# Gathering the rows of an expert as half rows on 128 partitions, and turning them with four transposes

## The chip, the cores and the metric

The kernel runs on one core of a Trainium2 chip, in float32. The metric is the device time of one execution in microseconds. The time before is the median of three executions.

## What is computed

One transformer block over 512 tokens of width 1024: a mixer (attention and a recurrent branch), and then a mixture of 32 experts, from which each token uses two. Only the second half is touched by the change:

```python
group_sel = jnp.argmax(group_logits, axis=-1)
top_p, top_i = lax.top_k(jax.nn.softmax(in_group, axis=-1), TOP_K_IN_GROUP)   # 2 of the 8 experts of a group
...
for e in range(N_EXPERTS):                                                     # 32
    hid = jax.nn.silu(t @ w_up1[e]) * (t @ w_up3[e])                           # 1024 -> 512, twice
    y = y + combine[:, e:e + 1] * (hid @ w_down[e])                            # 512 -> 1024
return y.reshape(b, s, d)
...
x = x + gt2 * rmsnorm(y, norm_gains[l, 3])
```

The weights of one expert are 6.3 MB (two matrices of 1024x512 and one of 512x1024), 201 MB for all of them.

## The kernel before

**Blocks.** The expert part works in blocks of at most 64 tokens (CAP) of one expert; with these inputs there are 32 blocks, one for each expert, and up to 18 more would be run if an expert had more than 64 tokens. There are three sets of buffers for the weights (u = 0, 1, 2), used in turn. Three blocks are written out, a loop `Fori` runs three blocks in each pass, and the last two are written out again.

**Weights.** SP issues all weight loads on one queue. The loads of the block three further on are issued when the block that holds the buffers has passed them: first halves at `up_half`, second halves at `up_done`, and the down matrix at `down_done` (L476, L480, L484). The first sets are issued ahead of the routing, the last three pieces of set 2 (L550, L551) after `rows_moved`, which stands for the rows of block 0.

**Rows.** When a tile of 128 tokens is ready, ACT scales it (L1031) and stores it into a buffer in DRAM, `h2_dram`, 512 rows of 1024 floats. The rows of block 0 are picked by matmuls with a one-hot matrix (L2168) and copied by ACT and DVE into `hrow[0]`. For every other block POOL gathers the 64 rows with an indirect DMA (`gather_rows`, L668) into `hrow[u]`, 64 partitions of 1024 floats; the indices are in `idx_i`. An index out of bounds leaves its row as it is, so a block with 20 tokens gathers 20 rows. The gather for the block three further on is issued when PE has turned the rows that are in the buffer (`hg_done`).

**Turning.** `turned(u)` (L2189) brings the rows to 128 partitions of the model's width with eight transposes, each of 64 rows by 128 columns (every eighth column of a row), into PSUM bank 0; DVE scales and shifts the eight pieces into `hgT` (L1503). PE does this for the next block between the up matmuls (L2211) and the down matmuls (L2230) of the present one. The outputs go back to token order by matmuls (L2195), which DVE adds to `acc` (L1544).

**End.** After the last blocks but two, SP loads `h2_dram` back (L590), 128 partitions by 1024 floats for each of four tiles. ACT (L1069) and POOL (L698) multiply it by the standard deviation in place, which gives x1 again; POOL (L702) and DVE add it to the outcome, and SP stores it.

## Time and profile before

| | us |
|---|---|
| median of three executions | 1099.11 |
| lowest, highest | 1097.51, 1099.91 |
| span of the profiled execution, first to last instruction | 1095.7 |
| PE busy in it | 1028.6 |
| DVE busy | 665.0 |
| ACT busy | 326.2 |
| POOL busy | 167.4 |

The profile gives the span of the profiled execution and not its whole time; the median of the timed executions lies 3.4 us above the span. PE's busy time is that of modelled ends of pipelined matmuls, so it doesn't say that PE is at its limit. What matters beside it is the busy share of the 16 DMA engines in each stretch and the GB/s that they moved.

### The profile page before, as it was taken

To read this page: it belongs to the slowest core of one execution; us is meant where nothing else is said; L and a number is where in the kernel's file an instruction comes from. 1 tells how busy PE (TensorE), PEld (TensorE's weight loads), DVE (VectorE), ACT (ScalarE), POOL (GpSimd) and SP (SyncE) were. 2 spreads that over 40 slices of the span, in tenths; PEclk is the share of its full clock that TensorE was granted. 3 is DMA by queue.
4 is the path that set the end of the run, shared out by engine and by line. 5 is a ranking of instruction groups with operands and counts; after the bars stand their busy time and mean duration, and the time that the engine had idled before them with its cause. 6 is when DMAs were issued, how large, how long until landed. Compare 5 with 4: busy or idle time off the path is not lost.

```text
span 1095.7 us, 18202 instructions
## 1 busy us (share of the span) xinstructions
PE 1028.6 (94%) x7403; PEld 591.1 (54%) x7403; DVE 665.0 (61%) x1131; ACT 326.2 (30%) x500; POOL 167.4 (15%) x220
## 2 busy tenths in 40 slices
PE   3999999999999999999998999999999999889895
PEld 1588588755557677768884444444334333333332
DVE  2478768444457443238347777777776665666666
ACT  4342462366652223365351111111111101110114
POOL 0100000322220011264500200000000000001003
PEclk9999999999999999999999999999999999999998
DMA  9676303205320004243439999999999999999994
GB/s 342 245 242 217 136 28 127 77 13 180 115 77 2 3 4 157 72 155 123 172 122 407 376 396 401 400 402 399 407 404 408 404 404 395 405 396 402 411 423 196
DMA packets 67732, 275.22 MB, mean 251 GB/s; under 512 B 7742, under 2 KB 17256, under 8 KB 43098
## 3 DMA queue, kind: packets, MB, share of 16 engines
q1 hardware_dynamic: 62976, 263.84, 62.4%
q10 hardware_dynamic: 2218, 6.52, 1.6%
q0 software_dynamic: 2480, 4.01, 1.3%
q8 instruction: 46, 0.75, 0.3%
q14 instruction: 12, 0.10, 0.0%
HBM read 274.26 MB, written 4.21 MB: 254 GB/s over the span
## 4 chain that ended last, share of the span: by engine, by line
PE 45%; SPq 25%; DVE 13%; DMA 7%; ACT 5%; issue 3%; POOL 1%; DVEq 0%; ACTq 0%
SPq L476 17%; PE ps L2211 8%; SPq L480 5%; PE ps L2230 4%; PE ps L1878 3%; DMA ring<-in_w_in 3%; DMA arena<-in_w_up 2%; SPq L484 2%; PE ps L2195 2%; PE ps L1859 2%; DMA arena<-in_w_mod 2%; PE ps L1867 2%; PE ps L1979 2%; PE ps L1860 1%; PE ps L1861 1%
## 5 line engine op out<-in xcount | busy, mean ns | idle before, releaser
L1544 DVE TENSOR_TENSOR arena<-arena,ps 128x1024 f32<-128x1024 f32 x124 | 145.5, 1215 | 52.9 <-PE ps L2195 52.9
L2211 PE MATMUL ps<-arena 128*64 128x512 f32 x672 | 152.9, 596 | 12.0 <-DMA arena<-in_w_up 11.2
L2211 PEld LDWEIGHTS ps<-arena 128*64 128x64 f32 x672 | 47.5, 137 | 105.5 <-issue 99.8
L1054 ACT ACTIVATE results<-ps,ST 64x512 fp32r<-64x512 f32 x64 | 43.8, 685 | 182.8 <-PE ps L2230 182.4
L2211 PE MATMUL ps<-ring,arena 128*64 128x512 f32 x352 | 79.9, 597 | 6.9 <-DMA ring<-in_w_up 5.5
L1047 ACT ACTIVATE arena<-ps 128x256 f32<-128x256 f32 x32 | 12.3, 385 | 234.7 <-PE ps L2211 234.7
L1720 PE MATMUL ps<-h_upper,w_upper 128*128 128x512 f32 (+1 forms) x184 | 73.7, 401 | 4.8 <-POOL h_lower_first L604 4.6
L2230 PE MATMUL ps<-arena 128*64 128x512 f32 x336 | 76.7, 598 | 1.3 <-DMA arena<-in_w_down 1.3
L1554 DVE SCALAR_TENSOR_TENSOR results<-ps,ST,results 64x512 fp32r<-64x512 f32 x64 | 48.0, 749 | 47.4 <-ACT results L1054 46.9
L2195 PE MATMUL ps<-results,back 128*128 128x512 f32 x248 | 73.7, 419 | 0.0
L1722 PE MATMUL ps<-h_upper,w_lower 128*128 128x512 f32 (+1 forms) x184 | 72.1, 392 | 0.0
L1503 DVE TENSOR_SCALAR arena<-ps,par 128x64 f32<-128x64 f32 x256 | 67.1, 335 | 0.1
L2195 PEld LDWEIGHTS ps<-results,back 128*128 128x128 f32 x248 | 42.1, 190 | 30.6 <-issue 23.5
L1867 PE MATMUL ps<-arena,ring 128*128 128x512 f32 x128 | 56.9, 597 | 0.0
L690 POOL COPY ST<-ST 128x1 f32 x27 | 4.9, 182 | 331.6 <-DVE results L1554 331.6
L2211 PEld LDWEIGHTS ps<-ring,arena 128*64 128x64 f32 x352 | 23.8, 137 | 57.3 <-issue 43.0
L1721 PE MATMUL ps<-h_lower_first,w_upper 128*128 128x512 f32 (+1 forms) x138 | 54.3, 394 | 0.0
L2230 PEld LDWEIGHTS ps<-arena 128*64 128x64 f32 x336 | 22.9, 136 | 44.6 <-issue 37.5
L2189 PEld LDWEIGHTS ps<-cst,arena 64*128 64x128 f32 x256 | 30.6, 200 | 24.5 <-issue 24.3
L1720 PEld LDWEIGHTS ps<-h_upper,w_upper 128*128 128x128 f32 (+1 forms) x184 | 34.3, 186 | 15.5 <-issue 6.7
L613 POOL TENSOR_SCALAR_AFFINE_SELECT arena<-arena 128x128 f32<-128x128 f32 x64 | 32.3, 537 | 66.2 <-DVE arena L1249 48.4
L2230 PE MATMUL ps<-ring,arena 128*64 128x512 f32 x176 | 40.2, 598 | 1.4 <-DMA ring<-in_w_down 0.9
(424 smaller groups left out, 1866.7 us busy)
## 6 DMA issues: line engine op xcount, KB each, us to landing
arena<-in_w_up SPq DMA_DIRECT2D x84, 1024.0 KB, 28.1
ring<-in_w_up SPq DMA_DIRECT2D x44, 1024.0 KB, 27.7
ring<-in_w_down SPq DMA_DIRECT2D x11, 2048.0 KB, 32.4
arena<-in_w_down SPq DMA_DIRECT2D x11, 2048.0 KB, 31.4
arena<-in_w_down SPq DMA_DIRECT2D x20, 1024.0 KB, 27.2
ring<-in_w_mod SPq DMA_DIRECT2D x6, 2048.0 KB, 9.1
arena<-in_w_mod SPq DMA_DIRECT2D x6, 2048.0 KB, 9.5
ring<-in_w_in SPq DMA_DIRECT2D x6, 2048.0 KB, 8.4
```

The lines of the kernel that those rows point to most:

```text
L476: eng.dma_start(eset_up[u][i][:, 2048 * m:2048 * m + 2048], src).then_inc(w_in_sem[u][m], 16)
L480: eng.dma_start(dst, src).then_inc(w_in_sem[u][m], 16)
L1503: last = TS(hgT[:, k, :], ps[:, 0, CAP * k:CAP * k + CAP], V("A1", k), V("SH1", k), ALU.mult, ALU.add)
L1544: TT(two_banks(acc[:, t, :]), two_banks(acc[:, t, :]), ps[:, BACK_BANK[t]:BACK_BANK[t] + 2, :], ALU.add).then_inc(back_added, 1)
L1554: last = STT(yo[o:o + HD, h:h + 512], ps[a:a + HD, DOWN_BANK, :], weight[a:a + HD, :], yo[a:a + HD, h:h + 512].bitcast(F32), ALU.mult, ALU ...
L1720: mm(ps[0:m_, b, :], hi, h_hi[:, k, :], start=(k == 0), stop=False)
L1721: used = mm(ps[0:m_, b, :], hi, h_lo[k], start=False, stop=False)
L1722: last = mm(ps[0:m_, b, :], lo, h_hi[:, k, :], start=False, stop=(k == KD - 1))
L1867: last = mm(ps[:, bank, :], w[:, k, P * (n % 2):P * (n % 2) + P], hT[:, k, :], start=(k == 0), stop=(k == KD - 1))
L2195: ins = mm(ps[:, bank + h, :], back[:, u, P * t:P * t + P], yo[:, 512 * h:512 * h + 512], start=True, stop=True)
L2211: last = mm(ps[64 * hf:64 * hf + 64, UP_BANK, :].rearrange("p (m n) -> p m n", m=2), hgT[:, k, :], up_pair(u, k)[:, :, 256 * hf:256 * hf + ...
L2230: last = mm(ps[64 * hf:64 * hf + 64, DOWN_BANK, :], hv2[:, k % 2, k // 2, :], wd[:, k % 2, 512 * hf:512 * hf + 512], start=(k == 0), stop= ...
```

## The change

`h2_dram` is stored in half order: the model's column 8p + 4g + j stands at place 512g + 4p + j of its row, so that each row is two half rows of 512 floats, g = 0 and g = 1. A gather reads 128 half rows, those with g = 0 into partitions 0 to 63 and those with g = 1 into 64 to 127; the index of a half row is twice the token's number, plus g. A block's rows are then 128 partitions by 512 floats, and are turned by four transposes of 128x128. The copy into `h2tok`, the one-hot matmuls for block 0 and the copies behind them follow the order, and the end reads the order back. A constant of one column (`nohalf`) is added, and one clearing of 128x1024 on POOL is left out. Loads of weights, waits and semaphores stay.

```diff
-        idx_i = sb("idx_i", [CAP, MAXB], I32)
-        idx_now = sb("idx_now", [CAP, NSET], I32)
+        idx_i = sb("idx_i", [P, MAXB], I32)
+        idx_now = sb("idx_now", [P, NSET], I32)
...
-        hrow = [S(14, 1)[0:CAP, 0:D], S(14, 1)[0:CAP, D:2 * D], S(13, 1)[0:CAP, D:2 * D]]
+        hrow = [S(14, 1)[:, 512 * u:512 * u + 512] for u in range(NSET)]
+        by_halves = lambda a: a.rearrange("t (p g j) -> t g p j", g=2, j=4)
+        h2_halves = h2_dram.rearrange("t (g n) -> (t g) n", g=2)
...
-        x1_rows = [S(i)[:, 0:D] for i in (0, 1, 15, 16)]
+        h2_rows = [S(i)[:, 0:D] for i in (0, 1, 15, 16)]
+        x1_rows = [S(i)[:, D:2 * D] for i in (0, 1, 15, 16)]
+        h2_by_column = [a.rearrange("t (g p j) -> t p g j", g=2, j=4) for a in h2_rows]
+        x1_by_column = [a.rearrange("t (p g j) -> t p g j", g=2, j=4) for a in x1_rows]
...
                 nc.gpsimd.indirect_dma_start(
-                    out=hrow[u], out_offset=None, in_=h2_dram, in_offset=bass.IndirectOffsetOnAxis(ap=index, axis=0),
-                    bounds_check=T - 1, oob_is_err=False).then_inc(hrow_in[u], 16)
+                    out=hrow[u], out_offset=None, in_=h2_halves, in_offset=bass.IndirectOffsetOnAxis(ap=index, axis=0),
+                    bounds_check=2 * T - 1, oob_is_err=False).then_inc(hrow_in[u], 16)
...
-                nc.gpsimd.tensor_scalar(x1_rows[t], x1_rows[t], std2[:, t:t + 1], None, ALU.mult).then_inc(x1_back, 1)
+                nc.gpsimd.tensor_scalar(x1_by_column[t], h2_by_column[t], std2[:, t:t + 1], None, ALU.mult).then_inc(x1_back, 1)
...
-                link(A(h2tok[:, t % 2, :], x1[:, t, :], ACT.Copy, scale=V("rs", 8 + t)))
+                link(A(h2tok[:, t % 2, :].rearrange("t (g p j) -> t g p j", g=2, j=4), by_halves(x1[:, t, :]), ACT.Copy,
+                       scale=V("rs", 8 + t)))
...
-                    A(x1_rows[t], x1_rows[t], ACT.Copy, scale=std2[:, t:t + 1]).then_inc(x1_ready, 1)
+                    A(x1_by_column[t], h2_by_column[t], ACT.Copy, scale=std2[:, t:t + 1]).then_inc(x1_ready, 1)
...
-                    last = TS(hgT[:, k, :], ps[:, 0, CAP * k:CAP * k + CAP], V("A1", k), V("SH1", k), ALU.mult, ALU.add)
+                    at = P * (k % 4) + CAP * (k // 4)
+                    last = TS(hgT[:, k, :], ps[:, 0, at:at + CAP], V("A1", k), V("SH1", k), ALU.mult, ALU.add)
...
-                    last = mm(ps[CAP * h:CAP * h + CAP, 0, :], picked[:, t, :], x1[:, t, 512 * h:512 * h + 512], start=(t == 0), stop=(t == NT - 1))
+                    last = mm(ps[CAP * h:CAP * h + CAP, 0, :], picked[:, t, :], by_halves(x1[:, t, :])[:, h], start=(t == 0), stop=(t == NT - 1))
...
-                hv = hrow[u].rearrange("p (q k) -> p k q", k=KD)
-                for k in range(KD):
-                    last = tr(ps[:, 0, CAP * k:CAP * k + CAP], hv[:, k, :], ident[0:CAP, 0:CAP])
+                hv = hrow[u].rearrange("s (p j) -> s j p", j=4)
+                for j in range(4):
+                    last = tr(ps[:, 0, P * j:P * j + P], hv[:, j, :], ident)
```

On POOL's queue this is the place from the clearing ahead of the first gathers to the clearing of `acc` behind them. Line numbers of the kernel before; `arena` holds `hrow`, and `h_rows` is `h2_dram`.

```order
L662 MEMSET arena 128x2048
L663 MEMSET arena 128x1024
L668 DMA arena<-h_rows,idx_i 64x1024 x2
L675 TENSOR_LOAD nblk_i
L675 ISA x2
L678 MEMSET arena 128x2048
L679 MEMSET arena 128x2048
```

In the changed kernel the same place reads as follows, with its own line numbers (five to seven higher).

```order
L668 MEMSET arena 128x2048
L673 DMA arena<-h_rows,idx_i 128x512 x2
L680 TENSOR_LOAD nblk_i
L680 ISA x2
L683 MEMSET arena 128x2048
L684 MEMSET arena 128x2048
```

Nothing changed its place: one clearing is gone, and each gather has 128 rows of 512 floats where it had 64 rows of 1024. It is the same in the loop and for the last two blocks.

On PE's queue this is the start of block 0, with the turning for blocks 0 and 1, in the kernel before; `results` holds the outputs of an expert.

```order
L2168 MATMUL ps<-arena 64x512 x8
L2176 MATMUL ps<-arena 64x50 x16
L2189 MATMUL ps<-cst,arena 128x64 x8
L2249 MATMUL ps<-key_diagonals,cst 128x512 x2
L2211 MATMUL ps<-ring,arena 64x512 x16
L2241 MATMUL ps<-SAs,arena 64x50 x16
L2189 MATMUL ps<-cst,arena 128x64 x8
L2218 MATMUL ps<-cst,arena 128x128 x2
L2230 MATMUL ps<-ring,arena 64x512 x8
```

And in the changed kernel, with its own line numbers (seven higher):

```order
L2175 MATMUL ps<-arena 64x512 x8
L2183 MATMUL ps<-arena 64x50 x16
L2196 MATMUL ps<-cst,arena 128x128 x4
L2256 MATMUL ps<-key_diagonals,cst 128x512 x2
L2218 MATMUL ps<-ring,arena 64x512 x16
L2248 MATMUL ps<-SAs,arena 64x50 x16
L2196 MATMUL ps<-cst,arena 128x128 x4
L2225 MATMUL ps<-cst,arena 128x128 x2
L2237 MATMUL ps<-ring,arena 64x512 x8
```

Only the two turnings differ: eight transposes to 64 columns each are four to 128 columns each, at the same place.

## Rows read from the trace of the kernel before

**Rows 1.** The page, part 2: the span in 40 equal slices, 27.4 us each.

```profile
DMA  9676303205320004243439999999999999999994
GB/s 342 245 242 217 136 28 127 77 13 180 115 77 2 3 4 157 72 155 123 172 122 407 376 396 401 400 402 399 407 404 408 404 404 395 405 396 402 411 423 196
```

**Rows 2.** Busy time by stretch: length, PE, PEld, DVE, ACT, POOL, clock, DMA share, GB/s.

```profile
640.00:840.00 200.00, 200.00 (x936) 82.14 (x936) 144.43 (x265) 24.57 (x42) 18.30 (x42) 1.00 1.01 402
840.00:1010.00 170.00, 154.02 (x704) 62.31 (x700) 108.74 (x192) 18.91 (x32) 14.14 (x32) 1.00 1.02 403
1020.00:1060.00 40.00, 38.54 (x180) 16.10 (x178) 25.79 (x48) 3.90 (x7) 0.00 (x0) 1.00 1.01 422
```

**Rows 3.** Waits of PE from 600 to 1070 us: us in total, times, longest.

```profile
PE ps L2211 <- DMA arena<-in_w_up: 11.2, 11, 1.8
PE ps L2211 <- DMA ring<-in_w_up: 5.5, 10, 1.2
```

**Rows 4.** The chain that ended last, two blocks in turn: start us, us, what.

```profile
629.69 3.43 PE ps L2211 x16
...
643.82 3.43 PE ps L2211 x16
```

**Rows 5.** The DMA view of the run: gather queue (packets, MB, share of engines), gathers issued.

```profile
q0 software_dynamic: 2480, 4.01, 1.3%
...
arena<-h_rows,idx_now POOLq DMA_INDIRECT x27, 7.2
...
arena<-h_rows,idx_i POOLq DMA_INDIRECT x4, 7.6
```

**Rows 6.** The DMA view from 640 to 1010 us: the gather queue.

```profile
q0 software_dynamic: 1975, 3.07, 3.0%
```

**Rows 7.** Busy time by stretch around two gathers, and one stretch of small packets.

```profile
881.00:884.00 3.00, 3.00 (x19) 1.97 (x16) 1.28 (x4) 0.39 (x1) 0.00 (x0) 1.00 1.02 350
928.00:932.00 4.00, 3.82 (x22) 2.13 (x18) 2.25 (x7) 0.39 (x1) 0.00 (x0) 1.00 1.02 317
485.00:490.00 5.00, 4.80 (x15) 2.38 (x14) 2.79 (x5) 4.63 (x9) 4.92 (x4) 1.00 1.02 406
```

**Rows 8.** The DMA view of those two gathers: the gather queue.

```profile
q0 software_dynamic: 80, 0.03, 5.6%
...
q0 software_dynamic: 80, 0.25, 21.7%
```

**Rows 9.** The timeline, transposes on PE: start us, us, engine, line.

```profile
1042.05 1.09 PE L2189 MATMUL ps<-cst,arena 64*128 64x64 f32 x8
...
569.09 1.04 PE L2101 MATMUL ps<-cst,arena 128*128 128x128 f32 x8
```

**Rows 10.** The timeline ahead of block 0, and the DMA's rate behind it.

```profile
570.16 1.03 ACT L1026 ACTIVATE arena<-ps 128x1024 f32<-128x1024 f32 x1 [0.79 <-PE ps L2101]
571.08 1.14 ACT L1031 ACTIVATE arena<-arena,par 128x1024 f32<-128x1024 f32 x1
...
593.01 3.65 PE L2168 MATMUL ps<-arena 128*64 128x512 f32 x16 [1.44 <-DVE arena L1491]
...
597.55 0.80 SPq L550 DMA_DIRECT2D arena<-in_w_up  x2
...
599.00:600.00 1.00, 1.00 (x4) 0.38 (x2) 0.96 (x2) 0.00 (x0) 0.72 (x1) 1.00 0.98 344
```

**Rows 11.** The timeline of the end; in brackets idle time before, and its releaser.

```profile
1068.29 3.65 PE L2211 MATMUL ps<-arena 128*64 128x512 f32 x16
...
1078.27 5.68 POOL L698 TENSOR_SCALAR arena<-arena,ST 128x1024 f32<-128x1024 f32 x2 [64.91 <-DMA arena<-h_rows]
1079.37 1.15 ACT L1069 ACTIVATE arena<-arena,ST 128x1024 f32<-128x1024 f32 x1
...
1080.85 1.02 ACT L1073 ACTIVATE arena<-ps 128x1024 f32<-128x1024 f32 x1 [0.33 <-PE ps L2277]
...
1087.39 2.35 POOL L702 TENSOR_TENSOR arena<-arena 128x1024 f32<-128x1024 f32 x1 [1.10 <-DVE arena L1627]
```

More of the change, by code:

```diff
@@ L59 @@
            ("strictU", 64), ("inclU", 64), ("eye", 64), ("lvlL", 6 * 64), ("lvlU", 6 * 64),
-           ("iota64", 64), ("m64", 8), ("blk18", MAXO), ("dest", 8), ("slot", NSET + E - LOOPED)]
+           ("iota64", 64), ("m64", 8), ("blk18", MAXO), ("dest", 8), ("slot", NSET + E - LOOPED), ("nohalf", 1)]
 CONST = {}
@@ L113, in constants @@
     put("dest", np.concatenate([p + P * np.arange(4)[None, :] + T * ch - NOWHERE for ch in range(2)], 1))
+    put("nohalf", 2 * NOWHERE + p // CAP)
     put("slot", p % CAP + CAP * np.array([[0, 1, 2, LAST, LAST + 1]]))
@@ L589, in _ @@
             for t in range(NT):
-                sp.dma_start(x1_rows[t], h2_dram[P * t:P * t + P, :]).then_inc(h2_moved, 16)
+                sp.dma_start(h2_rows[t], h2_dram[P * t:P * t + P, :]).then_inc(h2_moved, 16)
             for t in range(NT - 1):
@@ L661, in _ @@
             pool.wait_ge(merged_ready, KD)
-            nc.gpsimd.memset(S(14), 0.0)
-            nc.gpsimd.memset(S(13)[:, D:2 * D], 0.0).then_inc(zeroed, 1)
+            nc.gpsimd.memset(S(14), 0.0).then_inc(zeroed, 1)
             pool.wait_ge(zeroed, 1)
@@ L1038, in _ @@
             act.wait_ge(table_done, 1)
-            A(hrow[0][:, 0:512], ps[0:CAP, 0, :], ACT.Copy).then_inc(rows_moved, 1)
+            A(hrow[0][0:CAP, :], ps[0:CAP, 0, :], ACT.Copy).then_inc(rows_moved, 1)
             act.wait_ge(route_ready, 1)
@@ L1507, in _ @@
             dve.wait_ge(table_done, 1)
-            CP(hrow[0][:, 512:1024], ps[CAP:2 * CAP, 0, :]).then_inc(rows_moved, 1)
+            CP(hrow[0][CAP:2 * CAP, :], ps[CAP:2 * CAP, 0, :]).then_inc(rows_moved, 1)
             dve.wait_ge(table_done, 2)
             second, where = rt[:, 300:300 + MAXB], rt[:, 360:360 + MAXB]
-            link(TS(where, ps[:, 3, 0:MAXB], float(NOWHERE), None, ALU.add))
-            link(TS(second, where, float(T), -float(T), ALU.is_ge, ALU.mult))
-            TT(idx_i[:, :], where[0:CAP], second[0:CAP], ALU.add).then_inc(table_ready, 1)
+            link(TS(where, ps[:, 3, 0:MAXB], 2.0, K("nohalf"), ALU.mult, ALU.add))
+            link(TS(second, where, float(2 * T), -float(2 * T), ALU.is_ge, ALU.mult))
+            TT(idx_i[:, :], where, second, ALU.add).then_inc(table_ready, 1)
             ov = ovb
```

## The prediction

> **What bounds the kernel now.** I read the slices of the page first. From slice 22 (575 us) to the last but one, the DMA row stands at 9 and the rate near 400 GB/s, which it does nowhere else for long [rows 1]. This is the expert part, about half the span, and the gathers and the turning lie in it. So the second question is whether PE or the DMA engines set its pace, and the busy times by stretch answer that [rows 2]. From 640 to 840 us PE has no idle time at all, and a block takes 643.82 - 629.69 = 14.13 us [rows 4]; yet the 16 DMA engines are full too, with 402 GB/s. A block's 6.3 MB at 402 GB/s need 15.7 us. PE outruns the loads and lives on the sets that were loaded ahead. From about 840 us this lead is gone: PE idles 16 of 170 us, and its waits name the weight loads, 11.2 and 5.5 us in 21 waits [rows 3], while the DMA rate is the same 403. The page's PE row, near 10 tenths, would mislead here: the amount of data and the rate of the DMA engines set the time from 575 us to the last up matmuls at 1068.29 [rows 11]. Time that PE saves ahead of that turns into more waiting.
>
> Third, what sets the rate? With gathers in the stretch it is 402 to 403 GB/s, and from 1020 to 1060 us, behind the last gather, it is 422 with the same kind of loads [rows 2]. There is a cost in the gathers that their own bytes don't explain, since these are counted in the 402.
>
> **The cost of a gather now.** 640 to 1010 us holds 1975 packets of the gather queue and 3.07 MB [rows 6]. A gather has 80 packets [rows 8]: 64 rows, of which those out of bounds are tiny, and 16 more that I take to be completions, one for each DMA engine. That makes 24.7 gathers, with 3.07 MB / 4096 B / 24.7 = 30 rows each. The rate lost is (422 - 402) x 370 us = 7.4 MB, 300 KB for each gather. The run has 31 gathers [rows 5], so they cost 31 x 300 KB / 422 GB/s = 22 us beside their bytes. This is the sum that the change touches, and it can go either way.
>
> Two gathers of different filling split it [rows 7, 8]. Around the one with 0.03 MB (8 rows) the rate is 350 for 3 us: (422 - 350) x 3 = 216 KB lost. Around the one with 0.25 MB (62 rows) it is 317 for 4 us, 420 KB lost. So a row costs (420 - 216) / 54 = 3.8 KB beside its own 4.1 KB, and the 80 packets cost 216 - 8 x 3.8 = 186 KB, 2.3 KB each, whether they carry a row or not. For 30 rows this gives 186 + 114 = 300 KB, the same as the mean. It is two gathers only, so the split is an estimate.
>
> **The change, part by part.**
>
> Packets. A gather has 128 + 16 = 144 packets in place of 80. If the cost is one of packets, the first part becomes 186 x 144 / 80 = 335 KB, 149 KB more, and 31 x 149 KB / 422 GB/s = **+10.9 us**. If it is a cost of starting a gather, nothing is added. I take the first, since the small packets of a nearly empty gather already slow the loads for 2 us or more, which a cost of the start alone would not do.
>
> Rows. The 114 KB beside the bytes either go, since the data are spread over all partitions (-8.3 us for 31 gathers), or stay, being a matter of bytes, or double, being one of packets with data (+8.4 us). The cost beside the bytes (3.8 KB) is about the bytes themselves (4.1 KB): a row into 64 partitions is paid twice. The Trainium skill has a rule for that (SBUF — State Buffer, Door 1: The DMA port swizzle): a transfer to partitions 0 to 63 reaches only 8 of the 16 ports by which DMA writes, and one to 128 partitions all of them. The trace agrees in size, but no row shows which port a packet takes. By the rule alone the row cost would vanish; by the rows alone it lies anywhere between the ends. I take half of it gone, -4.2 us, the middle between gone and unchanged, because neither end has a row nearer to it.
>
> Small packets of data. 2 KB in place of 4 KB: a stretch in which every packet is 2 or 4 KB long moves 406 GB/s [rows 7] where 8 KB packets move 422, 4%. On 4.01 MB [rows 5] that is 0.4 us.
>
> PE. Eight transposes to 64 columns take 1.09 us; eight to 128 columns take 1.04 us [rows 9], so four take 0.5 to 0.7. That saves 0.4 to 0.6 us in each of 32 turnings, 13 to 19 us of PE's time, all of it under the DMA bound: 0 us. If that cover were gone, it would be worth the whole of it.
>
> Start. The ACT copy L1031 (1.14 us) reads in runs of 16 bytes, and the matmuls L2168 too. ACT's nearest row, L1026, goes between PSUM and SBUF in another order and takes 1.03 us for as many elements [rows 10]: 0. L2168 (3.65 us) gates `rows_moved` and so the issue at 597.55 (L550). The rate dips to 344 behind it, so the queue has run nearly dry, and a delay there would count. I take 0; the bounds are 0 and +3.65, twice its time. DVE's index steps are as long as before, in more partitions, and the clearing that goes was hidden.
>
> POOL. A gather's instruction may take longer for 128 rows. Behind it stand only the copies of indices and weights; the gather lands in 7.2 us [rows 5] and is wanted three blocks later, some 42 us. Covered, at any price in question. The first two gathers are wanted sooner, but PE has its lead then, and a PE delay is covered.
>
> End. L698 reads in runs on POOL: two take 5.68 us, and L702 has 1.10 us of room [rows 11]. If the strided reading made it half as slow again (2.8 us), some 1.7 us would reach the stores; if not, 0. ACT's L1069 has 0.33 us of room. I take +0.3. The Trainium skill (GPSIMD Engine Reference, 7. Performance pitfalls for Q7 kernels) gives half as much again for steps of more than 8 bytes. The steps here are of 4 bytes in runs of four, so the rule may not apply; no run shows it.
>
> Sum: 10.9 - 4.2 + 0.4 + 0 + 0.3 = +7.4 us. The profile gives no time of its execution beside its span of 1095.7; the median is 3.4 us above that, and I add the sum to the median: **1106.5 us**.
>
> **The rivals.** A difference of 0.2% (2.2 us) is about what this kernel's measurement can tell from none.
>
> *Spread gathers are cheaper (the other side).* The place is the DMA engines while a gather runs. Spreading over 128 partitions takes the row cost away, and the fixed part belongs to the gather and not to its packets: -8.3 + 0.4 + 0.3 = -7.6 us, 1091.5. It decides the sign where the added 64 packets cost less than 114 KB, 1.8 KB each. For it: the row cost is so near the row's bytes. Against it: the small packets of the nearly empty gather.
>
> *Every packet is dear.* Packets add 10.9 and data packets 8.4: with the small terms +20 us, 1119. For it: each packet of the gather queue comes between the 8 KB packets of the loads. Against it: the row cost fits bytes.
>
> *Nothing to be measured.* Fixed part and row cost stay, or the packets' +10.9 meets the whole -8.3: between +0.7 and +3.3 us, about 1100.5.
>
> *PE is the bound after all.* It has no idle time for the first 240 us of the blocks, and shorter turnings would let the loads be issued sooner. This asks for a DMA queue that is dry at times, and rows 2 show none: 13 us faster, 1086.
>
> **How the numbers follow.** Forecast case (packets cost, row cost partly gone, +3 to +12 us): 0.45, of which 0.03 fall within 0.2%. Every packet dear: 0.10. Nothing to be measured: 0.20, with 0.03 of it just slower. Cheaper: 0.21, from -3 to -9 us. PE: 0.04. So slower is 0.42 + 0.10 + 0.03 = 0.55, same 0.20, faster 0.25. The range runs from 1090.5, which holds nearly all of the cheaper case, to 1116, which leaves out the dear case: that and the PE case are 0.14, with some of the edges 0.2. The forecast case's own range is 1102 to 1111.
>
> **What would show it.** In the changed profile: a gather queue of 31 x 144 = 4464 packets and the same 4.01 MB; the stretch behind the last gather again at 422 GB/s; the stretch with gathers at about 395 to 400 instead of 402 (above 408 is the cheaper rival, under 392 the dear one); PE waits of L2211 on the loads of some 30 us and more; eight transposes replaced by four in 0.7 us or less; the last up matmuls some 7 us later than 1068.29. If L2168 takes over 4 us, or L698 over 7, the start or the end has its own part. The prediction is wrong if the fixed cost is one of the gather, which two gathers of 80 packets each can't tell from a cost of packets.

## The result and the profile after

The changed kernel takes **1080.84 us** (1079.76 to 1081.84) beside 1099.4 us for the kernel before on the same chip: a ratio of 0.9836, 95% interval 0.9824 to 0.9849. It is 18.6 us faster. (The two profiled executions differ by less, 1095.7 against 1079.1 us of span; see the chain below.) The prediction was 1106.5 us, with a range from 1090.5: it had the wrong sign, and the time lies outside the range.

The page of the changed kernel, parts 1 to 3: the busy time of PE, the DMA engines in 40 slices of 27 us, and the gather queue (packets, MB, share of the 16 engines' span).

```profile
span 1079.1 us, 17945 instructions
...
PE 1018.4 (94%) x7275; PEld 577.7 (54%) x7275; DVE 665.0 (62%) x1131; ACT 325.4 (30%) x500; POOL 168.4 (16%) x219
...
DMA  9666403203421004216427999999999999999994
GB/s 343 254 217 214 174 1 119 91 25 120 141 71 60 2 4 124 78 48 257 165 98 288 413 417 419 419 419 421 420 420 420 419 420 420 420 419 421 420 422 181
...
q0 software_dynamic: 2480, 4.02, 1.0%
```

Two things are to be seen. From slice 25 to slice 38 the rate is 419 to 421 GB/s where it was 395 to 411 [rows 1]. And the gather queue still has 2480 packets, for the same 4 MB [rows 5], though there are twice as many indices. 31 x (128 + 16) packets would be 4464. Two half rows therefore share one packet; the trace's packet records have 4096 bytes for nearly all of those that carry rows, as before.

Busy time by stretch (columns as in [rows 2]):

```profile
640.00:840.00 200.00, 196.12 (x879) 77.06 (x880) 144.07 (x262) 24.58 (x43) 19.15 (x42) 1.00 1.01 419
840.00:990.00 150.00, 145.73 (x652) 56.28 (x648) 106.86 (x193) 18.84 (x32) 13.81 (x31) 1.00 1.01 420
...
1000.00:1040.00 40.00, 37.29 (x166) 13.98 (x162) 26.75 (x45) 4.86 (x8) 0.00 (x0) 1.00 1.01 421
```

The rate with gathers in the stretch is now almost that behind the last one. From 640 to 1010 us it is 155.3 MB / 370 us = 419.7 GB/s (the two queues of the next rows and 0.04 MB of instructions). What a gather costs beside its bytes is (421 - 419.7) GB/s x 370 us / 27 gathers = 18 KB, where it was 300 KB; the rates are rounded, so this is good to some 7 KB. (The 27 are the 2160 packets of the next rows by 80.)

The DMA view from 640 to 1010 us, weight loads and gathers, answers to [rows 6]:

```profile
q1 hardware_dynamic: 20600, 151.87, 98.9%
q0 software_dynamic: 2160, 3.38, 2.5%
```

In the same view of the kernel before, the row of the weight loads is this one; that of the gathers is in [rows 6]:

```profile
q1 hardware_dynamic: 19768, 145.77, 98.5%
```

The share of the engines' time divided by the megabytes says how fast packets are. The weight loads went from 0.676 to 0.651% per MB, the rows from 0.98 to 0.74%. Both kinds of packet had taken longer while they ran side by side; without any gather the weight loads stand at 101.3% for 156.02 MB, 0.649% per MB (no_gather, below). The engines are full in both kernels; they get more done in the same time.

The chain that ended last (start us, us, what): two blocks in turn, and the last link of the blocks.

```profile
833.69 3.61 PE ps L2218 x16
847.80 3.61 PE ps L2218 x16
...
1024.42 27.31 DMA arena<-in_w_up
1051.78 3.68 PE ps L2218 x16
```

A block takes 847.80 - 833.69 = 14.11 us where PE leads, as before [rows 4], but it leads longer: the chain runs over PE to about 870 us, and the first wait of PE for a load comes at 971 us, where before it came at 842. The last up matmuls start at 1051.78 instead of 1068.29 [rows 11]. From the first block's start (601.94 before, 604.05 after) to there it is 466.35 us before and 447.73 after, 18.6 us less. The 2.1 us by which the first block starts later are scatter: the transposes L2108 (L2101 before) are already 2.0 us late at 577.29, and in a kernel that changes nothing ahead of them they are as late (upper_half, 577.23 against 575.25). These 2.1 us are also why the two profiled spans differ by 16.6 us and not by 18.6. Behind the last up matmuls there are 27.3 us to the end of the span, 27.4 before.

PE's waits from 590 to 1060 us (us in total, times, longest):

```profile
PE ps L2225 <- DVE arena L1586: 8.7, 31, 0.9
PE ps L2218 <- DMA arena<-in_w_up: 2.7, 4, 1.0
...
PE ps L2218 <- DMA ring<-in_w_up: 1.4, 4, 0.7
```

The waits on weights fell from 16.7 us [rows 3] to 4.1. The wait of L2225 is new in 31 blocks, and it is the time that the shorter turning saves: L2225 needs the product of DVE's L1586, which needs ACT's silu, and PE now gets there 0.3 us too soon.

The timeline of the turning, of the copy behind the start, and of the end (in brackets idle time before, and its releaser):

```profile
595.06 3.65 PE L2175 MATMUL ps<-arena 128*64 128x512 f32 x16 [1.44 <-DVE arena L1497]
...
599.58 0.75 PE L2196 MATMUL ps<-cst,arena 128*128 128x128 f32 x4
...
1061.79 5.69 POOL L703 TENSOR_SCALAR arena<-arena,ST 128x1024 f32<-128x1024 f32 x2 [64.11 <-DMA arena<-h_rows]
...
1062.85 1.15 ACT L1075 ACTIVATE arena<-arena,ST 128x1024 f32<-128x1024 f32 x1
```

L2175 was L2168, L703 was L698 and L1075 was L1069 [rows 10, 11]: reading in another order cost nothing on PE, POOL or ACT.

### The profile page after: what moved, and what is told of

It is laid out like the page before. It is cut to its first block, busy times and chain, and to the rows that moved or that the text cites. A ratio compares the mean times of both kernels' runs of the same rounds, so it can differ in the third digit from the quotient of the medians.

```text
span 1079.1 us, 17945 instructions
## 1 busy us (share of the span) xinstructions
PE 1018.4 (94%) x7275; PEld 577.7 (54%) x7275; DVE 665.0 (62%) x1131; ACT 325.4 (30%) x500; POOL 168.4 (16%) x219
## 3 DMA queue, kind: packets, MB, share of 16 engines
q0 software_dynamic: 2480, 4.02, 1.0%
## 4 chain that ended last, share of the span: by engine, by line
PE 54%; DVE 14%; SPq 14%; DMA 8%; ACT 6%; issue 2%; POOL 1%; DVEq 0%; ACTq 0%
PE ps L2218 13%; SPq L482 9%; PE ps L2237 7%; PE ps L2202 4%; DMA ring<-in_w_in 3%; PE ps L1885 3%; SPq L486 3%; DMA arena<-in_w_up 3%; PE ps L1866 2%; DMA arena<-in_w_mod 2%; PE ps L1874 2%; PE ps L1986 1%; PE ps L1867 1%; PE ps L1868 1%; PE ps L2127 1%
## 5 line engine op out<-in xcount | busy, mean ns | idle before, releaser
L1561 DVE SCALAR_TENSOR_TENSOR results<-ps,ST,results 64x512 fp32r<-64x512 f32 x64 | 48.0, 750 | 44.6 <-ACT results L1060 44.1
L2202 PEld LDWEIGHTS ps<-results,back 128*128 128x128 f32 x248 | 42.1, 189 | 30.7 <-issue 23.5
L1727 PEld LDWEIGHTS ps<-h_upper,w_upper 128*128 128x128 f32 (+1 forms) x184 | 34.4, 187 | 16.4 <-issue 7.4
L1729 PEld LDWEIGHTS ps<-h_upper,w_lower 128*128 128x128 f32 (+1 forms) x184 | 34.4, 187 | 8.2
```

Source lines behind the costliest of these rows:

```text
L1561: last = STT(yo[o:o + HD, h:h + 512], ps[a:a + HD, DOWN_BANK, :], weight[a:a + HD, :], yo[a:a + HD, h:h + 512].bitcast(F32), ALU.mult, ALU ...
L1727: mm(ps[0:m_, b, :], hi, h_hi[:, k, :], start=(k == 0), stop=False)
L1729: last = mm(ps[0:m_, b, :], lo, h_hi[:, k, :], start=False, stop=(k == KD - 1))
L2202: ins = mm(ps[:, bank + h, :], back[:, u, P * t:P * t + P], yo[:, 512 * h:512 * h + 512], start=True, stop=True)
```

## The experiments

Sixteen kernels, in the order of the questions that they answer. "Before" is 1099 to 1100 us in each comparison.

### What does a gather cost in all, and what does its being issued cost?

**no_gather**: the gather's issue is replaced.

```diff
-                nc.gpsimd.indirect_dma_start(out=hrow[u], ...)
+                pool.sem_inc(hrow_in[u], 16)
```

> The kernel before, with the 31 gathers left out: POOL only counts up the semaphore that each would have raised, so that blocks 1 to 31 work on whatever stands in the row buffers. Weights, turning and everything else are as before. This is the floor: if the 22 us that the trace puts on the gathers beside their bytes are real, the rate between 640 and 1010 us is 420 to 422 GB/s throughout, and the time is 22 us plus the 9.5 us of their own 4.01 MB lower, unless PE's 14.13 us for a block becomes the bound first: 1099.4 - 31.5 = about 1068, and not under about 1065. If the low rate had another cause (the cores of the chip beside this one, the memory), the rate stays at 402 to 405 and the time falls by less than 12 us.

**no_rows**: every index is out of range, so that each of the 31 gathers issues its 64 slots and carries nothing.

```diff
-            link(TS(where, ps[:, 3, 0:MAXB], float(NOWHERE), None, ALU.add))
+            link(TS(where, ps[:, 3, 0:MAXB], 1.0, K("off"), ALU.mult, ALU.add))
```

> The kernel before, with every index of the gathers out of bounds: each of the 31 gathers is issued, with its 64 tiny packets and 16 completions, and carries no row, so that blocks 1 to 31 work on stale rows. Left out is the data alone. My split (186 KB lost for the 80 packets, 3.8 KB for each row beside its bytes) gives 31 x 186 KB / 422 GB/s = 13.7 us above the kernel without gathers: about 1082, with the rate at about 410. If the fixed part is no cost of the packets but of the data that they carry, it lies within 3 us of the kernel without gathers, 1068 to 1071.

Measured: no_gather 1074.19 us, ratio 0.9769 (0.9753 to 0.9785); no_rows 1075.46 us, 0.9781 (0.9764 to 0.9798). Page and busy time by stretch of no_rows, and behind them one stretch of no_gather:

```profile
q0 software_dynamic: 2480, 0.01, 0.1%
```

```profile
640.00:840.00 200.00, 200.00 (x940) 82.41 (x936) 143.77 (x260) 24.90 (x43) 18.32 (x42) 1.00 1.01 421
840.00:980.00 140.00, 140.00 (x655) 57.27 (x653) 101.38 (x183) 17.13 (x29) 13.03 (x30) 1.00 1.01 421
```

```profile
640.00:840.00 200.00, 200.00 (x935) 82.62 (x936) 144.01 (x262) 24.47 (x42) 4.86 (x28) 1.00 1.01 422
```

All 2480 packets are there and the rate is 421 GB/s, beside 422 in no_gather. Packets that carry nothing cost next to nothing: 1.3 us of time, with intervals that overlap. The rate says the same, and it has to, since PE has no idle time here (200.00 of 200 us and 140.00 of 140) and so could hide a cost from the time: from 640 to 1010 us all queues moved 155.64 MB against 156.06 in no_gather, some 16 KB a gather less, not 186 KB. That takes away the fixed 186 KB per gather and nearly all of the term of +10.9 us with it. It is also why no_gather missed the 1068 us that it was to take: with PE always busy, the time can't fall as far as the loads would let it.

The 23.5 us between no_rows (1075.46) and before (1098.95) are paid for rows. 4.01 MB are 979 rows, 24.0 ns each, of which the bytes alone are 4096 / 422 GB/s = 9.7 ns. As no_rows is held by PE, this is the least that the rows cost the DMA engines.

### Is it the 128 partitions, the spread of the data, or the packets?

**wide_empty**: the kernel before, with gathers to 128 partitions whose upper 64 indices are out of range; whole rows on partitions 0 to 63, as before.

```diff
+    put("off", NOWHERE * (1 + p // CAP))
...
-        idx_i = sb("idx_i", [CAP, MAXB], I32)
+        idx_i = sb("idx_i", [P, MAXB], I32)
...
-                    out=hrow[u], ...
+                    out=hrow_wide[u], ...
```

> The kernel before with one thing changed: a gather is issued for 128 partitions of whole rows, the 64 real rows in partitions 0 to 63 as before, and 64 more in partitions 64 to 127 that are all out of bounds. The data, the bytes and the partitions that they go to are those of before, and so is the turning. Theory A (a gather for 128 partitions puts each row on the DMA engine that also brings the weights of that partition, a gather for 64 does not, and it is this mismatch that costs): the cost goes, 1080 to 1085, rate 418 or more. Theory B (the data must be spread over both halves of the partitions, since the 64 lower ones are reached by fewer paths): the row part stays and the packets of nothing are added, 1099 or more. Theory C (the half rows are cheap because two of them travel in one packet): no half rows here, so 1099 or more.

**wide_twice**: the same without the offset, so that the upper 64 partitions gather the same rows again (twice the bytes; the second copy isn't used).

> As the run before, but the upper 64 partitions gather the same whole rows once more, so that each gather carries twice the bytes, 8 MB in the run instead of 4, in packets of one whole row, on 128 partitions. Theory A: only the bytes cost, 4 MB / 422 GB/s = 9.5 us above the kernel with the upper half empty, about 1091 to 1094, rate (gathers included) 418 or more. Theory B: the same. Theory C (it is the pairing of half rows that helps): each packet costs as before, 2 x 22 us beside the bytes, over 1120, rate under 395.

**upper_half**: the 64 rows to partitions 64 to 127.

```diff
-        hrow = [S(14, 1)[0:CAP, 0:D], ...]
+        hrow = [S(14, 1)[CAP:P, 0:D], ...]
```

> The kernel before, with the row buffers in partitions 64 to 127 instead of 0 to 63; the gathers have 64 whole rows as before, and the turning reads them there. If 64 partitions are the trouble whichever they are (theories A and B), nothing changes: 1097 to 1101, rate 402. If it is the lower half alone, for instance since the gather's own list of packets is kept in memory that is reached by the same way, the cost goes or shrinks: under 1092, rate over 410.

**two_gathers**: the changed kernel, each gather issued as two, of the 64 first halves to partitions 0 to 63 and of the 64 second halves to partitions 64 to 127.

```diff
-                nc.gpsimd.indirect_dma_start(out=hrow[u], ... ap=index ...)
+                for g in range(2):
+                    nc.gpsimd.indirect_dma_start(out=hrow[u][CAP * g:CAP * g + CAP], ... ap=index[:, g, :] ...)
```

> The changed kernel, with each gather of 128 half rows issued as two gathers of 64 half rows, g = 0 into partitions 0 to 63 and g = 1 into 64 to 127. Data, bytes, places and turning are those of the changed kernel. Theory A (mismatch of row and DMA engine in a gather for 64): the whole cost is back, and as there are twice as many gathers it is up to twice the 22 us unless packets are paired: 1100 to 1125, rate under 405. Theory B (the data must be spread over both halves): they are, so it stays at 1081 to 1086, rate 415 or more. Theory C (half rows travel in pairs): 1081 to 1086 where they still do.

Measured, with the rate from 640 to 840 us:

| kernel | rows of a gather go to | MB, packets | us | ratio (95%) | GB/s |
|---|---|---|---|---|---|
| wide_empty | 0 to 63 of 128 | 4.02, 4464 | 1092.18 | 0.9931 (0.9913, 0.9949) | 420 |
| wide_twice | all 128, whole rows | 8.02, 4464 | 1091.87 | 0.9931 (0.9914, 0.9947) | 420 |
| upper_half | 64 to 127 alone | 4.01, 2480 | 1100.98 | 1.0014 (1.0001, 1.0028) | 401 |
| two_gathers | 64, then the other 64, half rows | 4.02, 2976 | 1098.05 | 0.9993 (0.9983, 1.0002) | 402 |

The rate falls wherever one gather has 64 destinations, whichever half they are in and whatever the size of a row, and nowhere else. wide_empty differs from before in nothing but the 64 empty places of each gather, so it is the cleanest test of this. wide_twice pays for little more than its bytes: 16.4 us over no_rows for 1958 rows, 8.4 ns each (PE hides a part), or 11.0 us over the changed kernel for the 979 rows that it moves more, 11.3 ns each. two_gathers differs from the change in the issue only, and all but 1.0 us of the old time is back (1099.03 there).

The expectations had three theories. B (the data must be spread over both halves) and C (half rows are cheap because they share packets) asked for wide_empty at 1099 or more and for two_gathers at 1081 to 1086; both fail. A (a gather for 128 partitions is cheap, one for 64 is not) has all the rates right, and the time of wide_empty wrong, which it had put at 1080 to 1085.

wide_empty has the rate and yet not the time. The busy time by stretch near its end shows where it is; the last two figures of a row are the share of the DMA engines that is busy and the rate.

```profile
1050.00:1060.00 10.00, 9.66 (x48) 4.05 (x50) 7.96 (x16) 0.75 (x2) 0.00 (x0) 1.00 0.86 334
1060.00:1070.00 10.00, 9.01 (x40) 3.50 (x41) 5.53 (x8) 2.52 (x4) 0.00 (x0) 1.00 0.44 183
```

From 1060 to 1070 us only 0.44 of the engines work, though loads still set the pace up to there: PE waits for one before the up matmuls at 1059.92, and its last up matmuls start at 1064.76, 13 us later than in the changed kernel. Some engines finish long before others. In the changed kernel the engines stop together, in the same two stretches:

```profile
1050.00:1060.00 10.00, 8.98 (x42) 3.49 (x40) 6.70 (x8) 1.67 (x2) 0.00 (x0) 1.00 0.88 360
1060.00:1070.00 10.00, 6.94 (x24) 3.03 (x20) 6.68 (x7) 7.99 (x16) 8.00 (x3) 1.00 0.02 9
```

If rows for partitions 0 to 63 all lie on eight engines, each of these has 4.0 MB / 8 of rows to move; evenly spread it would be 4.0 MB / 16. The excess, 4.0 MB / 16 at 422 / 16 GB/s, is 9.5 us, and 1092.18 - 1080.84 = 11.3 is near it. wide_twice agrees: it puts the same rows on the other half as well, so the busier engines have no more to do than in wide_empty, and with twice the bytes it takes the same time (1091.87). The packet records agree too: at most 7 packets with rows run at once in wide_empty, and 13 in wide_twice.

So the 18.6 us have two parts. Issuing the gather for 128 partitions brings back the rate and 6.8 us of the time (1098.95 to 1092.18); spreading the rows over both halves brings the other 11.3.

**wide_thirds** tests the theory of uneven engines: like wide_empty, but the rows of every third block go to the upper partitions (edit against wide_empty).

```diff
-    put("off", NOWHERE * (1 + p // CAP))
+    put("off", NOWHERE * (1 + ((blocks % NSET == 1) != (p >= CAP))))
```

> The kernel before with gathers to 128 partitions whose other half is out of range, like wide_empty, but the real rows of every third block lie on partitions 64 to 127, the others' on 0 to 63. In wide_empty all 4.0 MB of rows went to one half of the partitions, and if that half of the DMA engines carries them alone it has 4.0 MB / 8 engines against none on the other eight: 11 us over the 1081 of the change, measured 1092.2. Theory of uneven engines: here the lower half carries two thirds and the upper one, an excess of a third of what it was, so 1081 + 11 / 3 = 1084 to 1085. Rival, that whole rows to one half cost in another way (not by sums over the run): 1092, as wide_empty.

Measured: 1084.33 us, ratio 0.986 (0.9844 to 0.9877), 420 GB/s. The theory of uneven engines had named 1084 to 1085.

### Does PE's time matter?

**more_turning** puts three more transposes into each turning of the changed kernel (they are done again, and change no value); **less_turning** leaves four of the eight out of that of the kernel before, so that half of each turned row is old data.

```diff
-                for j in range(4):
+                for j in (0, 1, 2, 0, 1, 2, 3):
```

```diff
-                for k in range(KD):
+                for k in range(0, KD, 2):
```

> The changed kernel, with three of the four transposes of each turning done twice (seven in all), which gives PE back about the time that the turning took before, 1.1 us for 0.75. The DMA side is that of the changed kernel. If the gain is all in the gathers, and PE's shorter turning only turned into a wait for DVE and ACT, it stays within 1 us of the changed kernel: 1080 to 1082, PE period between 640 and 840 us within 0.1 us of 14.1. If PE's saving is part of the gain, it loses 31 x 0.35 = up to 11 us: up to 1092.

> The kernel before, with four of the eight transposes of each turning left out, so that half of the columns of every block are stale. It is the saving on PE alone (0.5 us or so for each block), with the gathers of before. If the DMA engines set the time, nothing changes: 1098 to 1100, with more waiting of PE on the loads. If PE's time counted, up to 31 x 0.5 = 15 us less, 1084.

Measured: more_turning 1081.19 us, 0.9844 (0.983 to 0.9857), beside 0.9836 for the change, with PE busy 200.00 of 200 us; less_turning 1099.78 us, 1.0012 (0.9997 to 1.0027). The fewer transposes are worth nothing that shows, in either kernel.

### Does it matter which slots carry the rows?

The engine that moves a packet isn't in the trace. The slots that carry rows can be chosen, though (a slot is the place of a row in its block, 0 to 63, and so its partition). In the seven kernels here the token of a slot is its number, and the slots not named are out of range. So the rows are not those that the experts should get, and with the slots the rows that are read from `h2_dram` change too; no run holds these fixed.

```diff
+    put("off", np.where(p % CAP < 2, p, 2 * NOWHERE))
...
-            link(TS(where, ps[:, 3, 0:MAXB], float(NOWHERE), None, ALU.add))
+            link(TS(where, ps[:, 3, 0:MAXB], 0.0, K("off"), ALU.mult, ALU.add))
```

The first three:

> The kernel before, but each of its 31 gathers carries two rows alone, those of slots 0 and 1 (4096 bytes each, 0.25 MB in all); the other 62 indices are out of range. The rows are not the ones that the experts' tokens need, so this leaves the right gathering out. Theory A (in a gather for 64 partitions a row is moved by another DMA engine than the one that writes the weights of that partition, and that mismatch costs): the rate falls where a slot is mismatched. In the traces rows next to each other in pairs share an engine; if slots 0 and 1 lie on the engine that also serves partitions 0 and 1, nothing is lost: rate 420 or more, time 1075 to 1077. If the cost is one of any gather for 64 partitions that carries rows at all (the fixed 186 KB of the prediction): 31 x (186 + 8) KB / 422 = 14 us over the 1075 of empty gathers, so 1085 to 1090, and the same for slots 2 and 3. If cost goes with the rows alone: 2 rows of 30 cost a fifteenth, 1076 to 1077, for both kernels.

> As slots_0_1, with slots 2 and 3 in the place of 0 and 1 (again two rows a gather, not the right tokens). Theory A in its strong form (pairs of slots dealt to the engines in turn, so that slots 2 and 3 lie on another engine than partitions 2 and 3): slower than slots_0_1, 1080 to 1090, rate 405 to 415 in the windows of the expert part. A fixed cost of any row-carrying gather: the same as slots_0_1, 1085 to 1090. Cost of rows alone: the same as slots_0_1, 1076 to 1077.

> The kernel before with all 64 slots of every gather valid, 64 rows of 4096 bytes to 64 partitions, 8.1 MB in all instead of 4.0 (the rows are not those of the right tokens). The 34 added rows a gather are 4.1 MB, 9.5 us at 422 GB/s. If the loss beside the bytes grows with the rows by the 3.8 KB a row of the prediction: 34 x 3.8 x 31 / 422 = 9.5 us more, 1118. If the loss is per gather and not per row: 1108 to 1109. If the mismatch is paid in proportion to all that a gather moves (22 us for 30 rows, so 47 us for 64): 1099 + 9.5 + 25 = 1134.

Measured: slots_0_1 1078.13 us, 0.9808 (0.9791 to 0.9824); slots_2_3 1078.58, 0.9811 (0.9795 to 0.9828); all_slots 1119.58, 1.0185 (1.0168 to 1.0202), at 391 GB/s from 640 to 840 us. The first two can't be told apart, and with 2 rows they carry too little to say why. They do rule out a fixed price of any gather that carries a row, which had asked for 1085 to 1090. all_slots costs 44.1 us over no_rows for 8.13 MB, 1985 rows: 22.2 ns a row. So the cost goes on with the rows, at 2.3 times that of the bytes. The 1118 us that the prediction's 3.8 KB a row had asked for are nearly met: the 1006 rows more than before cost 20.1 us, 19.9 ns each.

The other four carry 32 rows in each gather and differ in the slots alone (and so in which rows are read).

> The kernel before with slots 0 to 31 of every gather valid and 32 to 63 out of range (32 rows a gather, 4.06 MB in all, as before; they are not the right tokens' rows). If it does not matter which slots carry rows, 24 us over the 1075.5 of empty gathers, as before: 1099 to 1101. Theory A1 (slots dealt to the 16 engines four by four, so that slots 0 to 31 lie on engines that also write partitions 0 to 31): no mismatch, but all rows on eight engines, as in wide_empty: 1092. Theory A2 (dealt in pairs, slots 0, 1, 32 and 33 on the first engine): half of the rows mismatched, all engines loaded alike: 1099.

> The kernel before with slots 32 to 63 alone valid (32 rows a gather, not the right tokens' rows). Does not matter: 1099 to 1101, as low_slots. Theory A1: every row on an engine of the other half and all on eight engines, so slower than before and than low_slots by over 10 us: 1105 to 1115. Theory A2: 1099, as low_slots.

> The kernel before with slots 0 to 15 and 32 to 47 alone valid (32 rows a gather, not the right tokens' rows). Does not matter: 1099 to 1101. Theory A2 (pairs): these slots lie on the first eight engines, which write partitions 0 to 63: half of engines loaded but no crossing of halves: 1092, as wide_empty. Theory A1 (fours): half of the rows mismatched, engines loaded in two groups of four: 1099 to 1101.

> The kernel before with slots 16 to 31 and 48 to 63 alone valid (32 rows a gather, not the right tokens' rows). Does not matter: 1099 to 1101. Theory A2: all rows on the eight engines of the other half, mismatched and uneven: 1105 to 1115. Theory A1: as even_sixteens, 1099 to 1101.

| kernel | slots | us | ratio (95%) | GB/s, 640 to 840 |
|---|---|---|---|---|
| low_slots | 0-31 | 1094.11 | 0.9955 (0.9938, 0.9973) | 406 |
| high_slots | 32-63 | 1095.44 | 0.996 (0.9946, 0.9975) | 404 |
| even_sixteens | 0-15, 32-47 | 1111.71 | 1.0106 (1.009, 1.0123) | 398 |
| odd_sixteens | 16-31, 48-63 | 1126.23 | 1.024 (1.0223, 1.0257) | 383 |

The same bytes in as many packets cost 19 to 51 us over no_rows, by the choice of slots (and with them of the rows read). Busy time by stretch near the end of odd_sixteens, and the DMA view of it from 640 to 1010 us:

```profile
1080.00:1090.00 10.00, 10.00 (x50) 4.29 (x47) 5.99 (x9) 1.75 (x3) 0.00 (x0) 1.00 0.96 377
1090.00:1100.00 10.00, 10.00 (x46) 3.69 (x46) 7.58 (x15) 1.37 (x2) 0.00 (x0) 1.00 0.57 236
1100.00:1110.00 10.00, 9.06 (x38) 3.23 (x34) 5.96 (x8) 3.07 (x5) 1.63 (x1) 1.00 0.36 145
```

```profile
q1 hardware_dynamic: 18922, 139.58, 98.1%
q0 software_dynamic: 1920, 3.15, 3.4%
```

Both losses are there: the engines stop one after another (0.57, 0.36), and packets are slow while all work (0.703% per MB of weights where before has 0.676 and after 0.651). A small part of this execution's time is neither: the clock granted to PE stood at 0.90 and 0.76 in the two stretches from 1040 to 1060 us, behind a wait of PE, which is some 3 us of PE's work.

What follows. That it doesn't matter which slots carry rows is refuted, by 32 us. Theory A1, dealing in fours, asked for high_slots to be over 10 us slower than low_slots; they are 1.3 us apart, so it falls too. Theory A2, dealing in pairs (slots 0, 1, 32 and 33 on the first engine), is right that low and high are alike and that odd_sixteens is over 13 us slower than even_sixteens. It is wrong in the rest: low and high are 4 to 5 us faster than its 1099, and even_sixteens was to be the fastest of the four at 1092, since no row would cross from one half of the engines to the other, and it is 16 to 18 us slower than low and high. So halves are not what must match.
The packet records of the traces, with the start and duration of each packet, settle a part of this. At no moment of a gather are more than 19 packets with data in flight, for 16 engines, so the number of row packets in flight at once tells roughly how many engines carry rows. For the last column, weight packets are counted that start between the fifth and the fifth last row packet of a gather, from 640 to 1005 us.

| kernel | row packets in flight at once, at most | weight packets (8192 bytes) while rows move: mean ns, share over 350 ns |
|---|---|---|
| low_slots | 14 | 463, 90% |
| high_slots | 14 | 463, 88% |
| even_sixteens | 8 | 441, 94% |
| odd_sixteens | 8 | 544, 99% |
| before | 13 | 481, 96% |
| wide_empty | 7 | 316, 0.2% |
| changed kernel | 11 | 324, 0% |

In no_gather the mean is 314 ns, and 0.1% take over 350. The middle column speaks for pairs and against fours, which would put low_slots on eight engines and is refuted by 14. In slots_0_1 and slots_2_3 the two row packets of a gather never overlap, as if they had one engine. The last column speaks against the finer form: it has eight engines disturbed in even_sixteens and twelve in odd_sixteens, and yet nearly every weight packet is slow in both, so nearly all 16 engines are. What holds them all up during a gather to 64 partitions stays open.

The Trainium skill (DMA: Bandwidth & Descriptors, The descriptor swizzle) says that in a transfer to 128 partitions each engine writes one set of partitions of its own, four neighbours and the four that lie 32 further on, with 0 to 63 on the first eight engines. It leaves open how 64 rows are dealt. The wide kernels agree with it: wide_empty and wide_thirds lose time as if eight engines served each half (11.3 and 3.5 us). The finer form above takes its sets from there.

## Why the prediction was wrong, step by step

**The bound** was right. The DMA engines' rate sets the time: more_turning and less_turning change PE's work and not the time, and the 18.6 us lie in the expert part. The cost of the gathers beside their bytes was put at 22 us, and this was right in size too: of 300 KB for each gather 18 are left, 31 x 18 KB / 421 GB/s = 1.3 us, so some 20 us went from the DMA engines, and 18.6 came off the time.

**The step that failed is the split of the cost of a gather**, 186 KB for the 80 packets and 3.8 KB a row, and with it the term of +10.9 us. It stands under "Packets": "If the cost is one of packets, the first part becomes 186 x 144 / 80 = 335 KB, 149 KB more". It failed twice. The gather's packets did not become more (2480, not 4464), since two half rows share one. And packets that carry nothing have no price, as no_rows (421 GB/s with 2480 of them) and wide_empty (420 GB/s with 4464) show. The +10.9 us were 0, or about 1 by the rate of no_rows. The split came from two gathers with windows of 3 and 4 us, in which other loads also vary. The reason given for taking packets and not the start, that the small packets of a nearly empty gather slow the loads, was no reason: eight rows went along with them. By slots_0_1, two rows a gather cost 2.7 us in the whole run, at a rate of 421 GB/s, where 186 + 2 x 3.8 KB would have been 14 us. The last line of the prediction named only half of this: the fixed cost is one neither of the packets nor of the gather.

**Rows**, -4.2 us, was a mean between "gone" and "unchanged". Nearly all of the 300 KB belonged to the rows, the 186 KB as well, and nearly all went. The bound from below was wrong for the same reason: it let at most 8.3 of the 22 us go, so the range ended at 1090.5. Had both parts been let go, the sum would have reached 1099.1 - 22 = 1077, and the result would have been inside. The port rule that was weighed there (the Trainium skill, SBUF — State Buffer, Door 1: The DMA port swizzle) points the right way but isn't the whole cause: wide_empty puts its rows on partitions 0 to 63, as before does, and has 420 GB/s where before has 402. The 11.3 us that wide_empty loses at the end fit the rule as well as they fit eight busy engines; no run tells the two apart.

**Small packets of data**, +0.4 us: there are none, 0. What is left of the rows' price after the change is their bytes. It is 5.4 us over no_rows and not 9.5, because no_rows is bound by PE throughout (200.00 of 200 us), so a part of the bytes fits in beside it.

**PE**, 0, was right in what it adds to the time. The saving itself was put too high: 0.75 us for four transposes against 1.09 for eight is 0.34 us in each turning, not 0.4 to 0.6, and it became the wait of L2225. **Start**, 0, was right (L2175 takes 3.65 us as before; the first block's delay is scatter). **POOL** was right: a gather lands in 6.7 us, where it took 7.2 [rows 5]. **End**, +0.3, was 0: L703 takes 5.69 us where L698 took 5.68 [rows 11], so reading in runs of four elements cost nothing here.

**The rivals.** "Spread gathers are cheaper" had the place and the direction, at a chance of 0.21, but gave 1091.5 because it kept the fixed part. Of what the prediction said would show it, "above 408 is the cheaper rival" came true, with 419. "PE is the bound after all" gave 1086, nearer to the number and for a wrong reason. PE leads longer now, but as a consequence of the faster loads; more_turning gives its time back and nothing changes.

**What stays open.** That a gather to 64 partitions is what costs is shown; why it is slow is not. The trace has no engine numbers, and the mismatch of engine and partition, even in its finer form, doesn't account for nearly all weight packets being slow. That before, with 979 rows, takes 5.7 us more than low_slots with 992 is not explained; the rows of its gathers vary (8 and 62 in [rows 8]), and in low_slots they don't, and are the same 32 neighbouring rows of `h2_dram` each time.

## What to carry to other kernels

When a gather runs beside loads that fill the DMA engines, compare the rate of all bytes with and without gathers in the stretch: where it is lower with them, 128 partitions as destinations, with rows cut in two if need be, can take the excess away (18.6 us here, for 4 MB). The rows should then be spread alike over both halves of the partitions in the run as a whole, since a full rate in the middle can hide engines that finish late (11.3 us in wide_empty). And where a cost is split into a part per packet and a part per row from two short windows, the range must let either part carry the whole.

## What the runs showed of the hardware

- A row of 4096 bytes gathered to 64 partitions beside saturated loads cost 22 to 24 ns of the kernel's time over no_rows (all_slots, before), to 128 partitions 8.4 ns over no_rows or 11.3 ns over the changed kernel (wide_twice); its bytes at 422 GB/s are 9.7 ns.
- While the rows of a gather to 64 partitions move, the 8192-byte packets of the weight loads take 481 ns in the mean, against 314 without a gather; beside a gather to 128 partitions they take 316 to 324.
- Out-of-range indices cost next to nothing: 64 a gather 1075.46 us, against 1074.19 without any gather, and 421 against 422 GB/s.
- Two half rows of 2048 bytes that are gathered in one instruction share a packet of 4096: 2480 packets in all for 31 gathers of 128 indices, 2976 for 62 gathers of 64 (two_gathers).
- With the same bytes and packets, the choice of the 32 slots of 64 that carry rows (and with it of the rows read) moved the kernel from 1094.11 to 1126.23 us.
